# The MLP's down projection as seven block products in place of eight

## What is computed

```
x = x + relu(RMSNorm(x) @ W1)^2 @ W2        # W1 (1024, 4096), W2 (4096, 1024)
y = RMSNorm(x)
```

## Time and profile before

| what | value |
|---|---|
| median of 3 runs | 3126.65 us (3126.02 to 3128.45) |
| the profiled execution's own time | 3127.74 us |
| its span in the profile | 3126.0 us |
| mean granted TensorE clock | 0.983 |
| TensorE matmuls busy | 96% |
| VectorE, ScalarE, GpSimd busy | 43%, 37%, 38% |
| MLP matmuls | 4608 of 512 columns, and 96 transposes |
| MLP, first up matmul to last down matmul | 2062.4 to 3117.1 us |

### The profile page before, as it was taken

One profiled execution on the slowest core, in us unless ns is written; L12 is line 12 of the kernel. 1 busy time (PEld: TensorE's weight loads), 2 busy tenths in 40 slices (PEclk: granted clock), 3 DMA queues, 4 the chain that ended last, 5 costly groups with the idle time before them and its releaser, 6 DMA issues. The chain is left out here.

```text
span 3126.0 us, 44278 instructions
## 1 busy us (share of the span) xinstructions
PE 2993.6 (96%) x17907; PEld 2451.2 (78%) x17907; DVE 1334.8 (43%) x1933; ACT 1152.9 (37%) x1932; POOL 1184.4 (38%) x777
## 2 busy tenths in 40 slices
PE   5999999999999969899998999979999999999998
PEld 4878787877888746788887887868888888888887
DVE  4233232312379968667664353122224232322323
ACT  4241413243144548566664122232232323333222
POOL 4221121212123240123200433456665666666764
PEclk8999999999999989999999999989999999999999
DMA  4434232433545375111103545332333233333331
GB/s 112 164 137 131 75 117 83 134 102 118 164 143 175 112 245 185 64 53 56 39 22 112 175 148 170 95 125 91 108 92 97 89 100 122 94 95 95 109 114 61
DMA packets 239594, 353.15 MB, mean 113 GB/s; under 512 B 32928, under 2 KB 186272, under 8 KB 239392
## 3 DMA queue, kind: packets, MB, share of 16 engines
q1 hardware_dynamic: 239392, 350.32, 34.6%
HBM read 263.71 MB, written 96.36 MB: 115 GB/s over the span
## 5 line engine op out<-in xcount | busy, mean ns | idle before, releaser
L102 PE MATMUL pj_acc<-u_hi,pj_w_hi 128*128 128x512 f32 x1464 | 576.2, 394 | 13.0 <-POOL u_lo L543 13.0
L2484 DVE TENSOR_TENSOR x_tm<-m_ps,x_tm 128x512 f32<-128x512 f32 x384 | 265.0, 691 | 744.1 <-PE m_ps L104 744.1
L104 PE MATMUL pj_acc<-u_hi,pj_w_lo 128*128 128x512 f32 x1464 | 571.7, 390 | 0.0
L103 PE MATMUL pj_acc<-u_lo,pj_w_hi 128*128 128x512 f32 x1464 | 571.2, 390 | 0.0
L537 POOL TENSOR_TENSOR pj_w_lo<-pj_w_raw,pj_w_hi 128x1024 fp32r<-128x1024 f32 x61 | 157.8, 2586 | 729.7 <-ACT pj_w_hi L586 729.7
L102 PEld LDWEIGHTS pj_acc<-u_hi,pj_w_hi 128*128 128x128 f32 x1464 | 275.7, 188 | 88.0 <-issue 18.2
L2361 POOL TENSOR_TENSOR m_w_lo<-m_w_raw,m_w_hi 128x1024 fp32r<-128x1024 f32 x96 | 237.8, 2501 | 263.0 <-ACT m_w_hi L2275 263.0
L104 PEld LDWEIGHTS pj_acc<-u_hi,pj_w_lo 128*128 128x128 f32 x1464 | 275.7, 188 | 58.2
L103 PEld LDWEIGHTS pj_acc<-u_lo,pj_w_hi 128*128 128x128 f32 x1464 | 275.9, 188 | 56.4
L102 PE MATMUL m_ps<-m_v_hi,m_w_hi 128*128 128x512 f32 x768 | 299.6, 390 | 2.4 <-DVE m_v_lo L2452 2.4
L102 PE MATMUL m_ps<-m_w_hi,m_h_hi 128*128 128x512 f32 x768 | 299.6, 390 | 0.0
(11 more groups left out here) (283 smaller groups left out, 5278.7 us busy)
## 6 DMA issues: line engine op xcount, KB each, us to landing
m_w_raw<-in_w_mlp_dram SPq DMA_DIRECT2D x48, 1024.0 KB, 5.4
m_w_raw<-in_w_mlp_dram SPq DMA_DIRECT2D x96, 512.0 KB, 3.6
proj<-pj_stage SPq DMA_DIRECT2D x61, 768.0 KB, 3.5
pj_w_raw<-in_w_in_dram SPq DMA_DIRECT2D x61, 512.0 KB, 5.1
mo_gate<-proj SPq DMA_DIRECT2D x24, 768.0 KB, 4.4
mo_w_raw<-in_w_out_dram SPq DMA_DIRECT2D x48, 256.0 KB, 2.6
rpb_bias<-pj_shut SPq DMA_DIRECT2D x48, 192.0 KB, 3.0
rpb_bias<-rpb_near SPq DMA_DIRECT2D x24, 384.0 KB
```

Source lines behind the costliest of these rows:

```text
L102: pe.matmul(out, w_hi, x_hi, start=first, stop=False)
L103: pe.matmul(out, w_hi, x_lo, start=False, stop=False)
L104: return pe.matmul(out, w_lo, x_hi, start=False, stop=last)
L2484: dve.tensor_tensor(xt, ps2[:, q % 4], xt, ALU.add).then_inc(added, 1)
```

## The change

In groups 0 to 13 of each block the down part is computed by a seven-product scheme on 2 by 2 blocks: the two hidden tiles, two halves of the tokens (256 each, `HB`) and two halves of the output columns (512). `STEPS` lists the products: (activation block, weight block, target). Blocks 3 to 6 of either side are sums and differences of the first ones, made by VectorE in `sums_h` and `sums_w2`. Each product has two token tiles (`half`) of one `mm3`. Its results go either straight to `x_tm`, or to three accumulators in SBUF (`kept`), or, for the product with target None, add up over the 14 groups in PSUM banks 6 and 7. At group 14 (`PLAIN`), `fix` adds the accumulators to `x_tm` in 16 VectorE instructions. Groups 14 and 15 compute down as before.

To make room and order: `w1_raw` has one tile (0.5 MB) in place of two, the w1 parts have two slots in place of four, the w2 parts are two slots of seven blocks with `w2_lo` in the memory of `w2_f`, `h_lo` in the memory of `h_f`; the square of h moves to ScalarE, the low part of h to VectorE; `load_w2` waits until the group that read the slot is done; the statistics lie in `spare`.

```diff
+    PLAIN = NG - 2
+    STEPS = ((0, 0, 0), (3, 3, 1), (4, 4, None), (5, 5, 2), (1, 1, (0, 0)), (6, 2, (0, 1)), (2, 6, (1, 0)))
+    FIXES = 16
...
-        w1_raw = s.sb("w1_raw", [KD, 2 * P])
-        w1_hi, w1_lo = s.sb("w1_hi", [4, KD, P], F32R), s.sb("w1_lo", [4, KD, P], F32R)
+        w1_raw = s.sb("w1_raw", [KD, P])
+        w1_hi, w1_lo = s.sb("w1_hi", [2, KD, P], F32R), s.sb("w1_lo", [2, KD, P], F32R)
+        w2_hi = s.sb("w2_hi", [2, 7, TB], F32R)
+        w2_f, w2_lo = s.over("w2_f", "w2_lo", [2, 7, TB], F32, F32R)
...
         # SP
-            def load_w1(gg):
+            def load_w1(m):
+                if m:
+                    sp.wait_ge(w1_lo_done, m)
+                n = m % (2 * NG)
+                sp.dma_start(w1_raw[:], w1_t[:, :, n * P:(n + 1) * P]).then_inc(w1_in, 16)
+
+            def load_w2(gg):
                 if gg:
-                    sp.wait_ge(w1_lo_done, 2 * gg)
...
+                    sp.wait_ge(w2_hi_done, 2 * gg)
+                if gg >= 2:
+                    sp.wait_ge(part_done, items(gg - 1))
...
                 if gg + 1 < GG:
                     load_w2(gg + 1)
-                if gg + 2 < GG:
-                    load_w1(gg + 2)
+                for m in (2 * gg + 5, 2 * gg + 6):
+                    if m < 2 * GG:
+                        load_w1(m)
...
         # ScalarE, in the loop over gg, m = 2 * gg + 2
+                if g + 1 < NG:
+                    high_h(gg)
+                    if m + 2 < 2 * GG:
+                        high_w1(m + 2)
+                    hidden(m)
                 if gg + 1 < GG:
                     high_w2(gg + 1)
+                if g + 1 < NG:
+                    hidden(m + 1)
+                    if g == PLAIN:
+                        high_h(gg + 1)
+                    if m + 3 < 2 * GG:
+                        high_w1(m + 3)
...
         # GpSimd
             def low_w2(gg):
+                b = gg % 2
+                parts = (slice(0, 3), slice(5, 6))
+                if gg % NG < PLAIN:
+                    pool.wait_ge(w2_sum, sums(gg + 1))
+                    parts = (slice(0, 3), slice(3, 7))
+                for n, sl in enumerate(parts):
+                    pool.wait_ge(w2_hi_done, 2 * gg + n + 1)
+                    pool.tensor_tensor(w2_lo[:, b, sl], w2_f[:, b, sl], w2_hi[:, b, sl].bitcast(F32), ALU.subtract).then_inc(w2_lo_done, 1)
...
+                g, m = gg % NG, 2 * gg + 4
+                if g + 1 < NG and m < 2 * GG:
+                    low_w1(m)
                 if gg + 1 < GG:
                     low_w2(gg + 1)
...
+                if m + 1 < 2 * GG:
+                    low_w1(m + 1)
...
         # TensorE
+                if g < PLAIN:
+                    for a, w, target in STEPS:
+                        for half in range(2):
+                            cols = slice(half * P, (half + 1) * P)
+                            at = h_hi[:, a, cols], h_lo[:, a, cols], w2_hi[:, b, w], w2_lo[:, b, w]
+                            if target is None:
+                                mm3(pe, ps[:, 6 + half], *at, g == 0, g == PLAIN - 1)
+                                continue
+                            if items(gg) + q >= 4:
+                                pe.wait_ge(added, items(gg) + q - 3)
+                            mm3(pe, ps2[:, q % 4], *at, True, True).then_inc(part_done, 1)
+                            q += 1
+                    return
...
         # VectorE
+            def sums_w2(gg):
+                f, have = w2_f[:, gg % 2], sums(gg)
+                for j in range(2):
+                    dve.wait_ge(w2_in[j], 16 * gg + 16)
+                dve.tensor_tensor(f[:, 3], f[:, 5], f[:, 0], ALU.subtract).then_inc(w2_sum, 1)
+                dve.wait_ge(w2_sum, have + 1)
+                dve.tensor_tensor(f[:, 5], f[:, 2], f[:, 5], ALU.subtract).then_inc(w2_sum, 1)
+                dve.tensor_tensor(f[:, 4], f[:, 2], f[:, 3], ALU.subtract).then_inc(w2_sum, 1)
+                dve.wait_ge(w2_sum, have + 3)
+                dve.tensor_tensor(f[:, 6], f[:, 1], f[:, 4], ALU.subtract).then_inc(w2_sum, 1)
...
+                if g < PLAIN:
+                    sums_h(gg)
+                    low_h(gg)
+                    if g + 1 < PLAIN:
+                        sums_w2(gg + 1)
+                elif g == PLAIN:
+                    for part in range(2):
+                        fix(bk, part)
+                    low_h(gg)
+                    for part in range(2, 8):
+                        fix(bk, part)
+                elif gg + 1 < GG:
+                    sums_w2(gg + 1)
```

More of the change, by code:

```diff
@@ L2248, in _ @@
             load_w2(0)
-            load_w1(1)
+            for m in (1, 2, 3, 4):
+                load_w1(m)
             for gg in range(GG):
@@ L2261, in _, with high_w1 @@
         def _(act):
[L2262 to L2268, removed]
+            def high_w1(m):
+                act.wait_ge(w1_in, 16 * (m + 1))
+                if m >= 2:
+                    act.wait_ge(up_done, m - 1)
+                act.copy(w1_hi[:, m % 2], w1_raw[:]).then_inc(w1_hi_done, 1)
@@ L2270, in high_w2 @@
             def high_w2(gg):
+                b = gg % 2
                 for j in range(2):
                     act.wait_ge(w2_in[j], 16 * gg + 16)
[L2273 to L2287, removed]
+                act.copy(w2_hi[:, b, 0:3], w2_f[:, b, 0:3]).then_inc(w2_hi_done, 1)
@@ new lines, in high_w2, with hidden @@
+                if gg % NG < PLAIN:
+                    act.wait_ge(w2_sum, sums(gg + 1))
+                    act.copy(w2_hi[:, b, 3:7], w2_f[:, b, 3:7]).then_inc(w2_hi_done, 1)
+                else:
+                    act.copy(w2_hi[:, b, 5], w2_f[:, b, 5]).then_inc(w2_hi_done, 1)
+            def hidden(m):
+                gg, j = divmod(m, 2)
+                act.wait_ge(up_done, m + 1)
+                if gg:
+                    act.wait_ge(hl_done, lows(gg))
+                f = rel[:, 2 * j:2 * j + 2].rearrange("p a n -> p (a n)")
+                act.activation(f, ps1[:, j], ACT.Relu).then_inc(relu_done, 1)
+                act.wait_ge(relu_done, m + 1)
+                act.activation(f, f, ACT.Square).then_inc(sq_done, 1)
@@ new lines, in fix @@
+            def fix(bk, part):
+                n0 = FIXES * bk
+                for half in range(2):
+                    x0, x1 = (x_tm[:, bk * TPB + 2 * i + half].rearrange("p (a n) -> p a n", a=2) for i in range(2))
+                    k1, k5, k7 = (kept[:, k, half] for k in range(3))
+                    if part == 0:
+                        if half == 0:
+                            dve.wait_ge(added, items(bk * NG + PLAIN))
+                        dve.tensor_tensor(x0[:, 0], x0[:, 0], k1, ALU.add).then_inc(fixed, 1)
+                    elif part == 1:
+                        dve.wait_ge(fixed, n0 + 1 + half)
+                        dve.tensor_tensor(k1, ps[:, 6 + half], k1, ALU.add).then_inc(fixed, 1)
+                    elif part == 2:
+                        dve.tensor_tensor(x0[:, 1], x0[:, 1], k5, ALU.add).then_inc(fixed, 1)
+                    elif part == 3:
+                        dve.tensor_tensor(x1[:, 1], x1[:, 1], k5, ALU.add).then_inc(fixed, 1)
+                    elif part == 4:
+                        dve.wait_ge(fixed, n0 + 3 + half)
+                        dve.tensor_tensor(k7, k7, k1, ALU.add).then_inc(fixed, 1)
+                    elif part == 5:
+                        dve.wait_ge(fixed, n0 + 5 + half)
+                        dve.tensor_tensor(x0[:, 1], x0[:, 1], k1, ALU.add).then_inc(fixed, 1)
+                    elif part == 6:
+                        dve.wait_ge(fixed, n0 + 9 + half)
+                        dve.tensor_tensor(x1[:, 0], x1[:, 0], k7, ALU.add).then_inc(fixed, 1)
+                    else:
+                        dve.tensor_tensor(x1[:, 1], x1[:, 1], k7, ALU.add).then_inc(fixed, 1)
```

169 lines of the change are left out of this document (113 added, 56 removed).

## The result

| | before | changed |
|---|---|---|
| median, us (4 runs each) | 3126.69 (3126.02 to 3128.45) | 3164.74 (3159.84 to 3170.81) |
| ratio | | 1.0119 [1.0106, 1.0132] |
| profiled execution: span, granted clock | 3126.0, 0.983 | 3163.3, 0.972 |
| MLP, first up to last down matmul | 2062.4 to 3117.1 | 2061.4 to 3153.9 |

The account below looks back on a forecast made before the run. TensorE's matmul stream was taken to bound the kernel. Removed matmuls (-57.1 us) and delays (+31.2, +3.1, +4.5, +10.2, +19.7, +10.4) summed to +22.0, forecasting 3149 us; range 3083 to 3190, likeliest 3133 to 3175.

Parts of the forecast that it names:

- What is removed: Down part of groups 0 to 13: 42 matmuls for 48, a group of 20.40 us, -57.1 us in all.
- The ring: w1 load, cast, low, w2 sums and lows: a cycle of 21.2 us against TensorE's 20.40, +31.2 us.
- Ring at 20.4 but block-end stalls: Rival: ordinary groups keep TensorE's pace, only block ends stall: 3117 us; chance 0.14.
- TensorE stays the bound: Rival: loads and sums fit under 20.40 us, most stalls vanish: 3083 us; chance 0.20 for 3075 to 3105.
- Its count of 39 groups: 13 groups in each of 3 blocks, every one stalling 0.8 us in its down part: +31.2 us.
- `final`: Groups 6 and 7 of blocks 1 and 2: GpSimd's low gets between two scalings, +5.1 a block, +10.2 us.
- The store: Not in the forecast's list of edges, so 0; w1's load was taken with nothing ahead of it.
- `fix`: Group 14: additions blocked by GpSimd end at 21.6 us, +6.8 in blocks 0 and 1, +6.1 in block 2, +19.7.
- The alternation "one instruction each": VectorE instructions with two SBUF inputs and GpSimd's block each other, waiters taking turns; used for `final` and `fix`.
- Last group of a block: Group 15 of blocks 0 and 1: late w2 delays casts, `high_v`, `low_v` and last transpose, +5.2 each, +10.4 us.
- Start: First groups of the MLP: w2 sums and casts ahead of w1 tile 2 delay the second up, +3.1 us.
- The clock: Rival: half clock after each of five stalls of 5 to 7 us, +10, 3159 us; no chance of its own.

Follow-up runs that it names:

- experiment 1: Changed kernel with SP issuing the w2 load one place earlier, ahead of the even w1 load: 3110.09 us, ratio 0.9947 to the kernel before.
- experiment 7: Changed kernel with the edits of experiments 1, 3, 4 (stores a group later), 5 and 6 together: 3099.39 us, ratio 0.9909 to the kernel before.
- experiment 10: Changed kernel with w2 load first, `final` and store one tile a group, each `high_v` behind its transpose, next `sums_w2` later: 3073.92 us, ratio 0.9828 to the kernel before.
- experiment 2: Changed kernel with the last of the four weight sums done three times: 3224.96 us, ratio 1.0317 to the kernel before.
- experiment 3: Changed kernel with one final scaling in each of groups 6 to 9, store after group 10: 3161.54 us, ratio 1.0113 to the kernel before.
- experiment 4: Changed kernel with one store after each of groups 9 to 12 in place of four after group 9: 3167.12 us, ratio 1.0126 to the kernel before.
- experiment 5: Changed kernel with the last 12 `fix` additions placed between the adds of group 14: 3165.16 us, ratio 1.0118 to the kernel before.
- experiment 6: Changed kernel with `high_v` ahead of the w2 casts in group 15 and next sums behind `low_v`: 3150.09 us, ratio 1.0075 to the kernel before.
- experiment 9: Changed kernel with `fix` additions as scalar_tensor_tensor, or as eight wide instructions of 1024 columns: 3161.46 and 3168.36 us, single executions.
- experiment 8: Changed kernel with each final scaling of 1024 columns split into two of 512: 3190.31 us, ratio 1.0195 to the kernel before.

## Why the prediction came out as it did

The forecast was on the right side, and 3164.74 lies in its range; the sum was 16 us low. That it came so near is in part luck: two terms were 26 us too high together, the others 42 too low. By its own steps:

- **What is removed**: right. Groups without stalls are 20.40 us (experiments 1, 7, 10), and -57.1 can be had nearly whole.
- **The ring**: right in every link. Load 4.2 for 4.0, sums behind the w1 low, 21.05 and 21.36 for 21.2, the wait in the down part and released by a `kept` add, mostly 0.4 to 1.1 us each. Experiment 1 shows it as the cause, 2 agrees. The rivals were wrong for the changed kernel. "Ring at 20.4 but block-end stalls" is what experiment 1 made of it, 3110 for its 3117, and experiment 10 comes out below the 3083 of "TensorE stays the bound".
- **Its count of 39 groups**: wrong. 25 ordinary groups lagged, for 22.5 us, not 35.7. Behind every larger stall the ring is ahead and the next groups are free or nearly so: two after `final`, three after the store. I added terms that replace each other. Experiments 3 and 4 show this from the other side.
- **`final`**: mechanism right, size wrong, 25.3 for 10.2. I let the ring give back half. The waits alone are 6.26 + 1.95 and 6.35 + 2.24 = 16.8, the other 8.5 are half clock. By experiment 1 most of this price belongs to the ring, not to `final`.
- **The store**: missed, 11.2. I wrote that nothing stands ahead of the loads, and looked at SP's queue for w1 and w2 alone. The store was there in the kernel before as well, where TensorE has no lag behind it.
- **`fix`**: this is the step that failed. I had "GpSimd is busy from 6.6 to 18.5", so that VectorE's additions end at 21.6, and the adds, `low_v` and the transpose wait for them. In the changed kernel the additions ran at 0.60 us each and ended 11.8 us after the last seven-product down (2375.82 to 2387.59), the 12 that I had given for no blocking; it was GpSimd that waited, 4.8 us. The lag of blocks 0 and 1 was near my 6.8 (6.7 and 6.9, of which 4.1 each are the wait) for another reason: w1's low, load and cast ahead of `high_v`. Experiments 5 and 10 show it, and it fits block 2, which has no `high_v` and no lag, where I had put 6.1. The wide form of experiment 9, in which GpSimd does come in, gives the stall of block 0 by the path I had described; so the path exists, and I had the wrong side waiting. Even there block 2 lags only 0.4. The alternation "one instruction each", which I took from the earlier trace rows for every pair of instructions, isn't general.
- **Last group of a block**: right to the row (w2 late, `high_v` behind its casts; experiment 6 removes it); waits of 6.3 and 6.0 for 5.2, plus 3.8 of half clock and 1.3 in the next up parts.
- **Start**: 6.6 for 3.1. I followed tile 2 of w1. Tile 3 is late too (the wait at 2084.21 is 1.80 us), since with one slot its load starts only when tile 2's low ends: 0.1 + 4.0 + 1.05 + 2.4 = 7.6 us against 5.44 of matmuls.
- **The clock**: a rival with +10 that I "only widened the range by". It happened behind ten stalls of the last four places, 21 us. Without it, if the stalls stayed, the changed kernel would be at about +16.5, not +37.8: this term alone is more than the miss of the sum. The other errors come to -5.6: ordinary groups -13.2 and `fix` -12.7, against the store's 7.1, `final`'s 6.6, the start's 3.5 and group 15's 3.1. I had argued that no such stall inside a busy stretch stands in the trace. That is a reason not to know, and the earlier trace rows did show what a stall leads to.

The Trainium skill, SBUF — State Buffer, section "Who interferes with whom", has the VectorE instruction with two SBUF inputs and GpSimd blocking each other fully. The runs agree that a waiter waits for whole instructions (1.46 for 0.69, 2.61 for 0.41, 12.23 for 2.8). The same section says that issue order and not the shape of the operation decides who blocks. For a single pair that fits; for a row it doesn't: in the changed kernel a GpSimd low that was already waiting stayed out while addition after addition started (7.22 for 2.4), and the wide form of experiment 9 made the same additions longer and half as many, and the waiting side changed with it (2.63 and 6.25 for GpSimd in place of 7.22 for one low, 3.42 and 4.52 for 1.22 on VectorE).

## What to carry to other kernels

When a change shortens the bound engine's work, work out the longest ring of slots and hand-offs first, and then each edge as lag against that ring: while the ring is longer than the group, stalls inside it replace each other and fixing one is worth nothing (experiments 3 and 4); once it is shorter, they go. A stall outside it, as at the last transpose, pays at once (experiment 6, 15 us). Look for the cheapest link (here the order of two loads on one queue, 55 us) before giving up a scheme. And price the half clock behind a long stall of TensorE, here 1.6 to 2.6 us each.

## What was not expected of the hardware

- A row of 512-column VectorE additions with both inputs in SBUF, 0.60 us from start to start, kept a waiting GpSimd instruction out for up to 4.8 us; six 1024-column ones did not (experiment 9), nor did four 512-column halves of `final` (experiment 8). What decides it is open.
- After stalls of 1.95 to 6.35 us in a stream at granted clock 1.00, matmuls came 0.43 us apart for three to five us at 0.50. In the traces of the changed kernel and the experiments all stalls of 2.86 us and more were followed by it, none under 1.95, and of the 41 between these only 19: one of 2.83, in experiment 6 at 2602.55, wasn't. What decides between them isn't shown.
- Four stores of 512 KB, issued ahead of a load of the same queue, cost it 3.6 us of issue and about 2 us of landing.
